# Unequal token chunks (384, 320, 352 columns) and weight slots 4352 bytes apart in a two-layer hybrid decoder step

## What is computed

```python
for l in range(DEPTH):                                   # DEPTH = 2
    h = rmsnorm(x, norm_mix[l]); p = h @ w_in[l]         # 1024 x 3780, columns shared out among mixers A, B, C, D
    mix = concat[A | B | C | D]                          # sparse, gated-linear, dilated attention, retention
    x = x + mix @ w_out[l]                               # 1024 x 1024
    h = rmsnorm(x, norm_ffn[l])
    x = x + (silu(h @ w_gate[l]) * (h @ w_up[l])) @ w_down[l]     # D_FF = 2816
y = rmsnorm(x, norm_final)
```

## Time and profile before

| | |
|---|---|
| median of 3 runs (lowest, highest) | 3433.92 us (3433.62, 3439.69) |
| profiled execution, span from first to last instruction | 3432.8 us |
| TensorE busy | 3276.2 us, 95% of the span, 21248 matmuls |
| TensorE weight loads busy (beside matmuls) | 2815.0 us |
| VectorE / ScalarE / GpSimd busy | 1827.9 / 515.8 / 326.0 us |
| mean granted TensorE clock | 0.973 |
| DMA | 261.93 MB, mean 76 GB/s |

### The profile page before, as it was taken

One profiled execution on the slowest core, in us unless ns is written; L12 is line 12 of the kernel. 1 busy time (PEld: TensorE's weight loads), 2 busy tenths in 40 slices (PEclk: granted clock), 3 DMA queues, 4 the chain that ended last, 5 costly groups with the idle time before them and its releaser, 6 DMA issues.

```text
span 3432.8 us, 54639 instructions
## 1 busy us (share of the span) xinstructions
PE 3276.2 (95%) x21248; PEld 2815.0 (82%) x21248; DVE 1827.9 (53%) x3381; ACT 515.8 (15%) x1015; POOL 326.0 (9%) x594
## 2 busy tenths in 40 slices
PE   7999999898999999999989999998889999999997
PEld 4569567766999999999955685767678999999997
DVE  3599953769353333333427999246775433333335
ACT  2200112144110000000121001131432000000001
POOL 4000240000000000000040003300000000000000
PEclk9999999889999999999999999997999999999999
DMA  8211354132111111111052114431321111111112
GB/s 266 59 43 38 107 158 157 75 118 90 50 38 41 47 47 53 37 47 52 25 162 62 37 32 148 152 116 75 118 102 37 50 39 49 44 44 50 50 44 94
DMA packets 119600, 261.93 MB, mean 76 GB/s; under 512 B 18805, under 2 KB 74118, under 8 KB 116662
## 3 DMA queue, kind: packets, MB, share of 16 engines
q0 software_dynamic: 40288, 129.06, 11.9%
q1 hardware_dynamic: 74530, 114.47, 9.8%
q10 hardware_dynamic: 4516, 14.76, 1.2%
HBM read 227.10 MB, written 35.60 MB: 77 GB/s over the span
## 4 chain that ended last, share of the span: by engine, by line
PE 90%; DVE 5%; issue 2%; ACT 2%; DVEq 0%; DMA 0%; ACTq 0%; SPq 0%; POOL 0%; POOLq 0%
PE PS L1171 14%; PE PS L1169 14%; PE PS L1167 14%; PE PS L707 13%; PE PS L836 5%; PE PS L713 5%; PE PS L1058 2%; PE PS L842 2%; PE PS L1193 2%; PE PS L1195 2%; PE PS L1194 2%; PE PS L807 2%; PE PS L729 1%; PE PS L768 1%; PE PS L788 1%
## 5 line engine op out<-in xcount | busy, mean ns | idle before, releaser
L1849 DVE TENSOR_SCALAR_CACHE_REDUCE U<-U,smu 128x384 bf16<-128x384 f32 (+6 forms) x448 | 484.3, 1145 | 6.1
L707 PE MATMUL PS<-Hn,WS 128*128 128x352 f32 x1536 | 461.3, 463 | 14.9 <-DVE Hn L1772 14.9
L707 PEld LDWEIGHTS PS<-Hn,WS 128*128 128x128 f32 x1536 | 294.2, 192 | 180.7 <-issue 21.3
L2246 DVE TENSOR_TENSOR U<-PS,U 128x352 f32<-128x352 f32 x132 | 69.0, 523 | 540.5 <-ACT U L1632 540.5
L452 POOL DMA_DIRECT2D WS<-wjobs x226 | 121.1, 536 | 2399.5 <-PE PS L1171 1469.4
L1171 PE MATMUL PS<-HNHR,WSR 128*128 128x352 f32 x1920 | 346.3, 322 | 0.0
L1167 PE MATMUL PS<-HNHR,WHR 128*128 128x352 f32 x1920 | 345.3, 321 | 0.0
L1169 PE MATMUL PS<-HnR,WHR 128*128 128x352 f32 x1920 | 345.3, 321 | 0.0
L1171 PEld LDWEIGHTS PS<-HNHR,WSR 128*128 128x128 f32 x1920 | 314.5, 188 | 0.0
L1169 PEld LDWEIGHTS PS<-HnR,WHR 128*128 128x128 f32 x1920 | 313.6, 188 | 0.0
L1167 PEld LDWEIGHTS PS<-HNHR,WHR 128*128 128x128 f32 x1920 | 313.6, 188 | 0.0
(11 more groups left out here) (286 smaller groups left out, 4344.6 us busy)
## 6 DMA issues: line engine op xcount, KB each, us to landing
WS<-wjobs POOLq DMA_DIRECT2D x163, 512.0 KB, 3.9
WS<-wjobs POOLq DMA_DIRECT2D x48, 384.0 KB, 3.3
Hn<-ckT SPq DMA_DIRECT2D x16, 896.0 KB, 7.9
U<-kT_pool SPq DMA_DIRECT2D x160, 64.0 KB, 1.9
xres<-U SPq DMA_DIRECT2D x2, 4224.0 KB, 15.3
U<-xres SPq DMA_DIRECT2D x4, 2112.0 KB, 8.0
U<-v_pool SPq DMA_DIRECT2D x128, 64.0 KB, 2.1
U<-v_pool POOLq DMA_DIRECT2D x128, 64.0 KB, 2.4
```

The costliest lines, as they stand in the source:

```text
L707: i = mm(PS[:, base + c, 0:CW], w[:, k, :], Hn[:, k, c * CW:(c + 1) * CW], start=k == 0, stop=k == KR - 1)
L1849: ts(flags[0:m, flag_at[i]:flag_at[i] + s.shape[1]], s, CANDF[0:m, i:i + 1], None, ALU.is_ge, ALU.add, accum_out=CNT[0:m, i:i + 1])
L2246: tt(out=x, in0=PS[:, 2 * (t % 3) + 1, 0:CW], in1=U[:, SIL + (t % 3) * CW:SIL + (t % 3 + 1) * CW], op=ALU.mult)
```

## The change

Two sets of constants change. The chunks are 384, 320 and 352 columns wide, beginning at columns 0, 384 and 704, which are bytes 0, 1536 and 2816 of a row (12 and 22 times 128). A weight slot is 1088 floats or 4352 bytes (34 times 128), in SBUF and in the HBM table. Rows stay 4224 bytes apart. Every use of `CW` follows; the tensors behind `WS` move up by 512 bytes. No transfer, no semaphore and no product is added or taken away; the number of columns in all is the same. One ScalarE copy out of PSUM that took two chunks at once becomes two.

```diff
-NCH, CW = 3, TT // 3
+NCH = 3
+CO = [0, 384, 704, TT]
+CL = [CO[c + 1] - CO[c] for c in range(NCH)]
...
-SLOT = 8 * 132
+SLOT = 1088
...
-HT = SIL + 3 * CW
+HT = SIL + TT
...
         def part(c):
 
-            return slice(c * CW, (c + 1) * CW)
+            return slice(CO[c], CO[c + 1])
...
-                                i = mm(PS[:, base + c, 0:CW], w[:, k, :], Hn[:, k, c * CW:(c + 1) * CW],
+                                i = mm(PS[:, base + c, 0:CL[c]], w[:, k, :], Hn[:, k, part(c)],
...
-                    out = PS[:, UNIT_AT[u % 8], 0:CW]
+                    out = PS[:, UNIT_AT[u % 8], 0:CL[c]]
...
-                            return HNHR[:, k, c * CW:(c + 1) * CW], HnR[:, k, c * CW:(c + 1) * CW]
+                            return HNHR[:, k, part(c)], HnR[:, k, part(c)]
...
-                                i = split_products(PS[:, 2 * (t % 3) + b, 0:CW], halves(j), x, KR)
+                                i = split_products(PS[:, 2 * (t % 3) + b, 0:CL[c]], halves(j), x, KR)
...
-                            o = k * TT + c * CW
-                            return HDHR[:, o:o + CW], HDLR[:, o:o + CW]
-
-                        split_products(PS[:, 3 * (m % 2) + c, 0:CW], halves(j), x, n).then_inc(dn_ps, 1)
+                            t = slice(k * TT + CO[c], k * TT + CO[c + 1])
+                            return HDHR[:, t], HDLR[:, t]
+
+                        split_products(PS[:, 3 * (m % 2) + c, 0:CL[c]], halves(j), x, n).then_inc(dn_ps, 1)
...
-                for c, b in enumerate((1, 3, 6)):
-                    copy(z1[:, 0, c * CW:(c + 1) * CW], PS[:, b, 0:CW])
-                copy(z1[:, 1, 0:2 * CW].rearrange("p (c w) -> p c w", w=CW), PS[:, 4:6, 0:CW])
-                copy(z1[:, 1, 2 * CW:TT], PS[:, 7, 0:CW])
+                for r, banks in enumerate(((1, 3, 6), (4, 5, 7))):
+                    for c, b in enumerate(banks):
+                        copy(z1[:, r, part(c)], PS[:, b, 0:CL[c]])
```

More of the change, by code:

```diff
@@ L666, in _ @@
             for s in range(2 * NCH):
[L667 removed]
+                ks, t = slice(4 * (s % 2), 4 * (s % 2) + 4), part(s // 2)
                 sp.wait_ge(nrm_done, s + 1)
@@ L1133, in head_mean_b @@
                             pe.wait_ge(as_os, 2)
-                        m = mm(PS[:, at[r][c], 0:CW], cst(C_BD, P), rows(ZB, 2)[:, r, part(c)], start=True, stop=True)
+                        m = mm(PS[:, at[r][c], 0:CL[c]], cst(C_BD, P), rows(ZB, 2)[:, r, part(c)], start=True, stop=True)
                 m.then_inc(g_mean, 1)
@@ L1141, in head_norm_d @@
                     for r in range(2):
-                        m = mm(PS[:, MEAN_AT[c] + r, 0:CW], cst(C_BD, P), mixd[:, r, part(c)], start=True, stop=True)
+                        m = mm(PS[:, MEAN_AT[c] + r, 0:CL[c]], cst(C_BD, P), mixd[:, r, part(c)], start=True, stop=True)
                     m.then_inc(g_mean, 1)
@@ L1147, in head_norm_d @@
                     for r in range(2):
-                        m = mm(PS[:, VAR_AT[c] + r, 0:CW], cst(C_BD, P), Hn[:, r, part(c)], start=True, stop=True)
+                        m = mm(PS[:, VAR_AT[c] + r, 0:CL[c]], cst(C_BD, P), Hn[:, r, part(c)], start=True, stop=True)
                     m.then_inc(g_mean, 1)
@@ L1623, in finish_d @@
                     act.wait_ge(g_mean, 5 + c)
-                    act.activation(z1[:, :, part(c)], pair(VAR_AT[c]), ACT.Ln, bias=EPSC)
+                    act.activation(z1[:, :, part(c)], pair(VAR_AT[c], c), ACT.Ln, bias=EPSC)
                 act.drain()
@@ L1768, in norm_rows_by @@
             def norm_rows_by(at, gain, c, half, done):
-                r = U[:, VAR[at] + c * CW:VAR[at] + (c + 1) * CW]
+                r = U[:, VAR[at] + CO[c]:VAR[at] + CO[c + 1]]
                 for q in range(4 * half, 4 * half + 4):
-                    i = stt(out=Hn[:, q, c * CW:(c + 1) * CW], in0=X[:, q, c * CW:(c + 1) * CW],
+                    i = stt(out=Hn[:, q, part(c)], in0=X[:, q, part(c)],
                             scalar=gain[:, q:q + 1], in1=r, op0=ALU.mult, op1=ALU.mult)
@@ L1789, in norm_split @@
                     for half in range(2):
-                        k, t = slice(4 * half, 4 * half + 4), slice(c * CW, (c + 1) * CW)
+                        k, t = slice(4 * half, 4 * half + 4), part(c)
                         v.wait_ge(nrm_hi, 2 * c + half + 1)
@@ L1998, in add_out @@
                         v.wait_ge(wo_ps, u + 1)
-                        xx = X[:, m, c * CW:(c + 1) * CW]
-                        tt(out=xx, in0=PS[:, UNIT_AT[u % 8], 0:CW], in1=xx, op=ALU.add).then_inc(wo_add, 1)
+                        xx = X[:, m, part(c)]
+                        tt(out=xx, in0=PS[:, UNIT_AT[u % 8], 0:CL[c]], in1=xx, op=ALU.add).then_inc(wo_add, 1)
                         if m == KR - 1:
@@ L2209, in finish_d @@
                     v.wait_ge(g_mean, 2 + c)
-                    stt(out=mixd[:, :, part(c)], in0=pair(MEAN_AT[c]), scalar=-1.0, in1=mixd[:, :, part(c)],
+                    stt(out=mixd[:, :, part(c)], in0=pair(MEAN_AT[c], c), scalar=-1.0, in1=mixd[:, :, part(c)],
                         op0=ALU.mult, op1=ALU.add).then_inc(g_cen, 1)
@@ L2254, in ffn_part @@
                         v.wait_ge(dn_ps, f * (3 * KR) + 3 * m + c + 1)
-                        xx = X[:, m, c * CW:(c + 1) * CW]
-                        tt(out=xx, in0=PS[:, 3 * (m % 2) + c, 0:CW], in1=xx, op=ALU.add).then_inc(dn_add, 1)
+                        xx = X[:, m, part(c)]
+                        tt(out=xx, in0=PS[:, 3 * (m % 2) + c, 0:CL[c]], in1=xx, op=ALU.add).then_inc(dn_add, 1)
                         if n == LASTR and m == KR - 1:
```

46 lines of the change are left out of this document (23 added, 23 removed).

## The result

The changed kernel is slower: 3451.35 us median of 16 runs (3446.15 to 3464.85) against 3436.4 us of 16 runs of the kernel before on the same chip (3433.43 to 3458.99). The ratio is 1.0042, with a 95% interval from 1.0031 to 1.0052.

The account below looks back on a forecast made before the run. TensorE, busy 3276.2 of 3432.8 us, was taken as the bound, so the distance between matmul starts decides. Terms -8.4 - 7.3 + 2.0 + 0.4 + 1.3 = -12.0 us gave about 3422 us, range 3412 to 3453.

Parts of the forecast that it names:

- Even starts, fp32r products: Gate, up and down products: equal parity of chunk and weight starts makes all fast, saving 8.4 us and 7.3 us.
- Memory of the pace: Feed-forward parts: a pace entered after a stop lasts; first chunk of each of eight parts charged, 1.3 us.
- The slow pace locks in: Rival, feed-forward products: every part begins slow and stays slow, 18.5 us more, 3452 us; chance 0.23.
- the wider chunk and small steps: Starts of layers and feed-forward phases, 2.0 us, plus the split ScalarE copy and other small steps, 0.4 us.
- Widths: Matmuls of 384 and 320 columns: 32 columns added and taken away cancel, so L707 and L836 give nothing.
- The floor for 320 columns: Rival, chunk 1's 3552 products: they would not get 13.3 ns shorter, 47 us more, 3469 us; chance 0.06.
- The pace is mixed: Rival, feed-forward products: chunks 0 and 1 at 160.8 ns, only chunk 2 fast, about 3436 us; chance 0.16.
- The change does nothing: Rival, fp32r products: the pace follows something that goes with chunk number, not address, 3436 us; chance 0.12.
- What the wider first chunk exposes: Layer and feed-forward phase starts: longer norm, rounding and slow first passes cost 2.0 us for two layers.
- The rule weighed: TensorE matmuls: starts N / 2.4 + 2.5 ns apart, 149.2 ns for 352 columns at any address; change only costs 2.4 us.

Follow-up runs that it names:

- e1: Weight slots alone moved to 4352 bytes, chunks of 352 columns as before, against the kernel before: 3449.51 us against 3439.56, ratio 1.0035.
- e3: Kernel before with slots 1088 floats apart and chunk 1 read from column 320, which computes something else: 3455.98 us, ratio 1.0044.
- e4: Kernel before with slots 1088 floats apart and chunk 1's k rows taken as 1 to 7, then 0: 3451.79 us, ratio 1.0042.
- e10: e4 plus three pairs of breaks in the k order in each part's first row: 3426.41 us against the kernel before's 3437.56, ratio 0.9961.
- e7: Changed kernel with the k rows of one run reordered in 15 places: one run, 3443.84 us against the kernel before's 3438.06.
- e11: e10 with the weight slots of the kernel before, 1056 floats apart: one run, 3433.17 us against the kernel before's 3442.48.
- e6: e4 plus one pair of breaks (4, 6) in the k order in each part's first row: 3443.88 us, ratio 1.0014 to the kernel before.
- e8: e4 plus one pair of breaks (0, 6) in the k order in each part's first row: 3433.49 us, ratio 0.9994 to the kernel before.

## Why the prediction was wrong

**What failed is the first step, "Even starts, fp32r products".** It took the pace as a function of the addresses: fast where chunk and weights are both even or both odd. That held in the 18 runs of the earlier trace rows, and it is no law. In e1 chunks 0 and 2 have just that condition and are slow; in e3 one part runs fast and seven slow at the same addresses, and e4 and e10 have the same addresses and opposite paces. The kernel before spoke against it too: in the earlier trace rows the run of chunk 2 at 1095.17 has rounded weights, so all is even, and took the 1.13 us of chunk 1 and not the 1.11 of chunk 0. In the six-row down phases of that trace none of chunk 2's 96 runs with rounded weights was fast, where the rule wants all. The prediction read from the earlier trace rows only that the mean lies above 158.3. The correlation in the earlier trace rows was real: in the kernel before, all gate and up rows behind a part's first repeat it. The reading that fits all runs is that the starts of chunk 1 and of the odd slots are the places where the stream was disturbed, and that there it changed state in a fixed way, row after row. What the prediction read as cause was the switch. It was to gain 8.4 and 7.3 us and cost 8.5 and 1.8 instead: gate and up phases went to 139.31 us, down phases to 69.81 busy.

**"Memory of the pace" had the right mechanism and 1.3 us for it.** The text said that a pace once entered after a stop lasts and that odd starts served to leave it, from the earlier trace rows; it then charged the first chunk of each part alone, though the change takes away just what ends that stretch. By its own sentence the charge had to run to the end of the part: 9504 products and not 384, or 32.3 us at 3.4 ns each, which turns its -12.0 into +19. Here the two steps contradicted each other, and the chance was given to the first.

**The rival "The slow pace locks in" named what happened, and its total is close in part by luck.** It gave 23.28 us for a row and 3452 us; the trace has 1018.98 - 995.77 = 23.21, and the median is 3451.35. But it put 12.8 + 3.3 us on the feed-forward stages and 2.4 on the wider chunk and small steps; the stages lost 10.55, and the rest of the 15 is not located. Its 69.85 us for a down phase leaves out the 0.16 of the last matmul's tail, so it stands against 69.65 and not 69.81; a phase that is slow throughout is busy for 70.00 us in e4. Products of 320 columns are 1.6 ns better than slow by 0.42 ns a column, which makes up the 0.07 us of the row. Its "against", that chunks of other widths might shake the pace, did not help: 352 and 320 columns ran at the slower of the two paces that e7 has for each, and 384 at the only one seen. That the 2.0 ns of the 384 columns are a locked pace too is thus not shown. The rival had 0.23; e1, e3 and e4 show that it was the rule and not the exception, and the range took it in. That stops "begin slow" is true for most entries and not for all: e3's first part and e10's second entered fast.

**"Widths" held.** Plain passes of 384, 320 and 352 columns start 322.5, 269.2 and 295.8 ns apart, as put (322, 269, 296), and L709's products are busy 460.9 us against 461.3. The floor for 320 columns is refuted by 1.17 us for eight (146.7 ns, below 150), and in e7 by 145.0. "The pace is mixed" expected chunks 0 and 1 above chunk 2; it is chunk 1 that is lower. "The change does nothing" fell with the interval of the ratio.

**"What the wider first chunk exposes", 2.0 us, can't be seen.** The wait ahead of layer 1's feed-forward part grew from 6.88 to 7.14 us, as put, but the part still begins 1.85 us earlier than before; the phases ahead of it differ from one execution to the next: over all the kernels here that part begins at 946.7 to 963.7 us. The lower end of the forecast's own range, 3413, is 3415.6 by the terms named for it (3421.9 - 2.9 - 2.4 - 1); nothing hangs on that. Suppliers stayed hidden: the waits of 1480.3 and 294.5 us stand against 1469.4 and 289.8.

**The rule weighed** (the Trainium skill, page TensorE: Matmul & The Clock Gate, section Part 2: What happens when you issue a matmul: weights and streamed operand have a port each, and starts lie N / 2.4 + 2.5 ns apart) agrees with no fp32r stream here. By it 352 columns would take 149.2 ns, an estimate, and took 158.3 or 161.7; 384 would take 162.5 and took 175.1; 320 would take 135.8 and took 145.0 to 146.8. The same section calls that distance the gap of an isolated matmul and says that in a stream of weight loads and matmuls both set it, which the prediction left out; it has no figure for fp32r.

What stays open: what in the chip holds the state. That it lies in how the weights' reads and the streamed row's reads fall against each other is a guess from e11 and from the parity of the starts; no run takes the two apart. Nor is it known why 384 columns show one pace, why a stop sometimes leaves a stream fast, or where the other 4 us between the medians lie.

## What to carry to other kernels

A back-to-back stream of matmuls can have two stable paces with the same code, addresses and clock; before putting a pace down to an address, look whether it changes at the address or stays changed behind it. An edit that makes a stream more regular also takes away what ended its bad stretches, so a cost that "lasts until something breaks it" must be charged to the new end, and here the more regular kernel lost 0.4%. Where a pattern of starts can be chosen freely, as by the order of the contraction, put one irregular stretch at each entry, read single distances in a trace for every state that the stream can enter with, and choose the sequence that ends well from each of them.

## What the runs showed of the hardware that was not expected

- fp32r products of 352 columns, each with a weight load, start 158.3 ns apart (156 and 160 in turn) or 161.7 (164, 165, 158, 159), at a granted clock of 1.00 in both, and keep their pace for as long as 1280 products (e3, layer 1's first part).
- Exchanging two k in a run of eight can change the state of all products behind it: 161.7 to 158.3 ns for the rest of a part, 2.8 us in a phase of 864 products (e6, 136.98 in a part where it did, 139.76 in one where it did not).
- What an exchange does depends on the state in front of it: (4, 6) led B to fast, A to A, fast to A; (0, 6) led A and B to fast and fast to slow, the same way in all parts of e6, e8 and e10 that met the case.
- Products of 320 columns have 145.0 and 146.7 ns, 384 columns only 175.1 (e7).
- Plain float32 products showed no such states: passes of 352 columns start 295 or 296 ns apart in both kernels, in the chunks that start odd as in those that start even (L707 and L709).
